# Each token's gate halves as two accumulating products of 128 columns, evicted by a copy

## What is computed

```python
gate = jax.nn.softmax(top_s.astype(F32), axis=-1).astype(h.dtype)
...
act = jax.nn.gelu(jnp.einsum('tkd,td->tk', u[ix], hx), approximate=False) * gx
return jnp.einsum('tk,tkd->td', act, v[ix])
```

## Time and profile before

| | |
|---|---|
| median of 3 runs | 3873.95 us (3873.43 to 3877.39) |
| the profiled execution's own time | 3893.15 us |
| its span, first to last instruction | 3891.5 us |
| TensorE matmuls busy | 3833.1 us, 98% |
| TensorE weight loads busy | 3308.9 us, 85% |
| VectorE busy | 2804.0 us, 72% |
| ScalarE busy | 1878.9 us, 48% |
| GpSimd busy | 1667.1 us, 43% |
| the two gate stages | 729.2 to 1101.0 us and 2714.4 to 3097.1 us |

### The profile page before, as it was taken

One profiled execution on the slowest core, in us unless ns is written; L12 is line 12 of the kernel. 1 busy time (PEld: TensorE's weight loads), 2 busy tenths in 40 slices (PEclk: granted clock), 3 DMA queues, 4 the chain that ended last, 5 costly groups with the idle time before them and its releaser, 6 DMA issues.

```text
span 3891.5 us, 60334 instructions
## 1 busy us (share of the span) xinstructions
PE 3833.1 (98%) x18945; PEld 3308.9 (85%) x18945; DVE 2804.0 (72%) x5198; ACT 1878.9 (48%) x3594; POOL 1667.1 (43%) x1769
## 2 busy tenths in 40 slices
PE   9998999999999999999999999999999999999998
PEld 7665888888888999999788888888888888999997
DVE  4647799778742688887777774998777724778876
ACT  3747433577743333335555553333777733333334
POOL 0311335778720566651200001436877702556641
PEclk9999999999999999999999999999999999999999
DMA  9547466555556899994588873334555656999972
GB/s 275 170 150 191 163 208 202 196 197 187 192 211 203 295 359 362 356 352 145 173 237 236 241 211 114 106 122 154 204 187 191 223 198 215 344 339 360 363 279 92
DMA packets 547288, 875.95 MB, mean 225 GB/s; under 512 B 40593, under 2 KB 384785, under 8 KB 543281
## 3 DMA queue, kind: packets, MB, share of 16 engines
q1 hardware_dynamic: 458688, 605.81, 47.8%
q0 software_dynamic: 51568, 201.04, 14.0%
q10 hardware_dynamic: 36864, 67.13, 4.6%
HBM read 745.57 MB, written 262.21 MB: 259 GB/s over the span
## 4 chain that ended last, share of the span: by engine, by line
PE 86%; issue 5%; DVE 4%; ACT 3%; POOL 1%; another core or an unknown queue 0%; DMA 0%; ACTq 0%; DVEq 0%; SPq 0%; POOLq 0%
PE ps L191 77%; PE ps L1768 2%; ACT first_scaled L1787 1%; DVE own_sum L1636 1%; POOL w_lo L176 1%; PE ps L2332 1%; PE ps L2311 1%; ACT w_hi L163 1%; PE ps L1269 1%; PE ps L2082 1%; DVE w_lo L169 1%; PE ps L614 0%; PE ps L615 0%; PE ps L600 0%; DVE gate_group L1697 0%
## 5 line engine op out<-in xcount | busy, mean ns | idle before, releaser
L163 ACT ACTIVATE w_hi<-w_raw 128x1024 fp32r<-128x1024 f32 x692 | 732.3, 1059 | 1209.7 <-PE ps L191 891.8
L169 DVE TENSOR_TENSOR w_lo<-w_raw,w_hi 128x1024 fp32r<-128x1024 f32 x583 | 717.2, 1230 | 670.2 <-ACT w_hi L163 539.9
L191 PE MATMUL ps<-h_hi,w_hi 128*128 128x512 f32 (+1 forms) x3072 | 1155.9, 376 | 18.2 <-DVE w_lo L169 7.9
L191 PE MATMUL ps<-h_hi,w_lo 128*128 128x512 f32 (+1 forms) x3072 | 1143.3, 372 | 0.0
L191 PE MATMUL ps<-h_lo,w_hi 128*128 128x512 f32 (+1 forms) x3072 | 1142.0, 372 | 0.0
L191 PE MATMUL ps<-y_hi,w_hi 128*128 128x512 f32 (+1 forms) x2368 | 871.4, 368 | 8.2 <-DVE w_lo L169 6.4
L191 PE MATMUL ps<-y_hi,w_lo 128*128 128x512 f32 (+1 forms) x2368 | 867.9, 367 | 0.0
L191 PE MATMUL ps<-y_lo,w_hi 128*128 128x512 f32 (+1 forms) x2368 | 867.3, 366 | 0.0
L191 PEld LDWEIGHTS ps<-h_hi,w_hi 128*128 128x128 f32 x3072 | 577.9, 188 | 110.6 <-issue 13.2
L191 PEld LDWEIGHTS ps<-h_hi,w_lo 128*128 128x128 f32 x3072 | 577.7, 188 | 82.2
L191 PEld LDWEIGHTS ps<-h_lo,w_hi 128*128 128x128 f32 x3072 | 578.1, 188 | 78.5 <-issue 2.2
(11 more groups left out here) (376 smaller groups left out, 3555.4 us busy)
## 6 DMA issues: line engine op xcount, KB each, us to landing
value_rows<-in_v SPq DMA_DIRECT2D x256, 512.0 KB, 5.9
w_raw<-in_u SPq DMA_DIRECT2D x256, 512.0 KB
w_raw<-in_v SPq DMA_DIRECT2D x256, 512.0 KB
acts<-gelu ACTq DMA_DIRECT2D x256, 256.0 KB, 2.2
gates<-gate_group POOLq DMA_DIRECT2D x28, 2048.0 KB, 8.0
blocks<-acts SPq DMA_DIRECT2D x256, 192.0 KB
blocks<-gates SPq DMA_DIRECT2D x96, 512.0 KB
w_raw<-in_od_in SPq DMA_DIRECT2D x65, 512.0 KB
```

The lines of the kernel that those rows point to most:

```text
L163: self.nc.scalar.activation(self.wh[:, slot % SPL, :], self.raw[:, slot, :], ACT.Copy).then_inc(self.sig("w_hi_ready").sem, 1)
L169: self.nc.vector.tensor_tensor(self.wl[:, slot % SPL, :], self.raw[:, slot, :], self.wh[:, slot % SPL, :].bitcast(F32), ALU.subtract).then ...
L191: ins = self.nc.tensor.matmul(out, a[:, s, w], b[:, k, :], start=first and j == 0 and m == 0, stop=last and j == n - 1 and m == 2)
```

## The change

Each token's product of 256 columns becomes two products of 128 columns, one for each half, which accumulate in the same 128 columns of PSUM (`start` on the first, `stop` on the second). The second half of each token's place in PSUM stays unused. VectorE's eviction copies these 128 columns a token in place of adding 2 x 128. The semaphores, their counts and their order stay as they are.

```diff
@@ -1694,8 +1694,8 @@
             dve.wait_ge(gm.sem, g * TS + gm.base + R + 4 * q + 4)
             if at == 0:
                 dve.wait_ge(gd[half].sem, g * 32 + gd[half].base + 16 * (1 + part // 2))
-            v.tensor_reduce(gb[:, half, :, at:at + 4].rearrange("p a t -> p t a"),
-                            self.bank(q).rearrange("p t c a -> p t a c"), AX_X, ALU.add).then_inc(gc.sem, 1)
+            v.tensor_copy(gb[:, half, :, at:at + 4].rearrange("p a t -> p t a"),
+                          self.bank(q)[:, :, 0, :]).then_inc(gc.sem, 1)
 
@@ -1765,9 +1765,9 @@
                     pe.wait_ge(gc.sem, g * self.Q + gc.base + q + 1)
                     for r in range(4):
                         t = (4 * q + r) % R
-                        ins = p.nc.tensor.matmul(self.bank(q)[:, r, :, :].rearrange("p c a -> p (c a)"),
-                                                 self.o2[:, t, :], self.os[:, t, :, :].rearrange("p c a -> p (c a)"),
-                                                 start=True, stop=True)
+                        for c in range(2):
+                            ins = p.nc.tensor.matmul(self.bank(q)[:, r, 0, :], self.o2[:, t, :], self.os[:, t, c, :],
+                                                     start=c == 0, stop=c == 1)
                     ins.then_inc(gm.sem, 4)
```

## The result

The changed kernel takes **3947.55 us** (median of 4 runs, 3946.45 to 3950.55) against 3873.69 us before (4 runs). The ratio is 1.019, with a 95% interval of 1.0178 to 1.0202: 73.9 us slower, inside the forecast's range and its narrower one, and 5 us under the forecast of 3953. The profiled execution took 3947.13 us, its span 3945.5.

What follows compares the result with a forecast made beforehand. TensorE was taken to bound both gate stages, with 2.8 us idle; +80.6 us for the products less 2 us of waits made +79, so 3953 us against the 3873.95 median; range 3942 to 4128, its own narrower one 3943 to 3967.

Steps and rivals of the forecast that it cites:

- A: Gate products on TensorE: the weight load sets the narrow products' pitch, +69 to +93 us; chance 0.60.
- The load's pitch: Gate products on TensorE: 1,536 at 112 ns, 172.0 us, less 91.4 today, +80.6 us.
- The unit behind the burst: Next unit's wide products on TensorE, behind the longer burst: cost taken as already counted, no term of its own.
- The waits: TensorE's waits for the eviction in the gate stages: at most 2.8 us of idle time returns, 2 us taken off.
- Sum: Whole kernel: 80.6 - 2 = +79 us, forecast 3953 us against the median of 3873.95.
- VectorE: Gate evictions: a copy at 700 ns in place of 1,216, 99 us of VectorE time saved, all beside TensorE.
- The upper bound, 1,216: Gate eviction on VectorE: the copy's time bounded by 683 ns below and today's 1,216 ns above.
- B: Narrow gate products cost like plain float32 products, 224 ns each, +253 us or +237; chance 0.20.
- C: Second gate product finds its weights in place and pays no load, not slower, 3871 us; chance 0.07.
- D: Gate products' loads hide in part under the product before, pitch 86 ns, +41 us, 3915 us; chance 0.08.
- the 81 ns: Trainium skill's price per product for a stream of loads and products at N=128, an estimate of +33 us.
- E: As A, and TensorE's clock gives way; half the bursts at the lower level cost 86 us more, 4039; chance 0.05.

Runs made afterwards that it cites:

- e9: Changed kernel, but each gate product loads only 64 of the 128 stationary columns, same products and moving columns; ratio 1.0007 to the kernel before.
- e3: Changed kernel with only the first-half product of 128 columns for each token, second half left out; ratio 0.998 to the kernel before.
- e5: Kernel before with each token's product of 256 columns done twice into the same place; ratio 1.0228 to the kernel before.
- e6: Kernel before with four products of 64 columns for each token, side by side, added as before; ratio 1.0909 to the kernel before.
- e2: Kernel before with the eviction copying the first half in place of adding both halves; ratio 1.0002 to the kernel before.
- e1: Kernel before with two products of 128 columns for each token, side by side, VectorE still adding the halves; ratio 1.0193 to the kernel before.
- e7: Changed kernel, but the eviction writes its 512 values side by side; ratio 1.0186 to the kernel before.
- e8: e1 reordered to first halves of four tokens, then second halves, so no neighbours share weights; ratio 1.0188 to the kernel before.

## Why the prediction was right, and where its sum was off

Direction, cause and size held: the split pays a second full weight load per token on the engine that bounds. Load-bound (A) it is by e9, e3, e5 and e6 together: the average distance in a burst of 16 is 107 to 108 ns at 64 and at 128 columns with a full load, 119 at 256, and 60 at 128 columns with half a load. Step by step:

- **The load's pitch.** Taken 112 ns from plain float32 rows, and inside a burst it is 112. But the first product of a burst loads under a wide one, so the averages are 108.5, and 105 in a burst of eight. A pass has 13 units with eight tokens and 6 with four, so the six passes of both layers take 6 x (13 x 1.735 + 6 x 0.84) = 165.6 us in place of my 172.0. The term was too large by 6.
- **The unit behind the burst.** Not in my sum: it takes 5.52 in place of 5.48 us in 114 units, +4.6 us. This is the same load again, spared at the head of the burst and paid behind it, so the two errors nearly cancel, and counting 112 ns for every product came out almost right without my having seen either.
- **The waits.** I gave back 2 us, capped at the 2.8 us of idle time, and called them the eviction's. With the chain's own pieces (60 units of 5.48, the decode stage's last one, 45.7 us of gate products) a stage of before is 380.0 us, and it took 382.8: 2.8 us of waits a layer, 5.6 in all, twice the idle time of the earlier trace rows. So my cap of 2.8 us was no bound. The weight loads show more waiting than the matmul row; in the first stage before:

```profile
PEld ps L1768 <- DVE gate_group L1697: 2.3, 5, 0.6
PEld ps L191 <- DVE w_lo L169: 1.1, 2, 0.6
...
PE ps L1768 <- DVE gate_group L1697: 1.0, 3, 0.4
```

The columns are us, times and the longest. A third of the loads' waiting is not for the eviction but for `w_lo`, VectorE's share of the big product. After, the same sum gives 419.3 and the stage took 419.1, without any such wait: all of it is gone. And it is not the copy that removed it. e2 gives 1.1 us in the first stage and 1.0 in the second, and keeps the wait for line 169, while e1, with the old eviction, has the changed kernel's stages. The waits vanish since TensorE itself comes later. A slower bounding engine takes up the waits that it had.

- **Sum:** 165.6 - 91.4 + 4.6 - 5.6 = +73.2 us, where the two stages grew by 72.7.
- **VectorE.** This step failed: 1,119 ns and not 700, 192 x 0.097 = 19 us spared and not 99 (in the windows of the two stages VectorE's busy time fell by 21 us, where the prediction named some 100 as a sign). I argued that the old eviction's time was that of its reads, so that its stride cost nothing. The strided writes of 512 values take 1,119 ns by themselves, so taking reads away could spare no more than 97; how long the reads of 1,024 would take with writes side by side no run shows. The upper bound, 1,216, was the nearer row. The Trainium skill has it, in "SBUF — State Buffer", section "Door 1: The DMA port swizzle": accesses to SBUF that each cross into a new 16-byte line pay a penalty. Here every write did, and e7 agrees (1,120 against 680 ns). It cost nothing, as VectorE is covered.

Of the rivals, B (the price of plain float32, 224 ns) is refuted by every narrow run, C by e8, D by the pitch of 112, on average 108.5, in place of 86; the 81 ns that the prediction set beside D are not what this stream shows either. E was no fact of this change but of e6.

## What to carry to other kernels

Count a matmul by its weight load as well as by its columns: with 128 stationary columns of this type a product costs its load, 112 ns here, as long as its moving columns take less. On the line through 60 ns at 128 and 119 at 256 columns that is up to about 240 columns, an estimate. So splitting a product that just covers its load nearly doubles its price (119 to 217 ns), and merging two such halves that share their stationary operand gives the 98 ns back. Before sparing an engine, add up the bounding engine's pieces over the stage and compare with the stage's length; that difference, here 2.8 us of 383, is all that sparing another engine can give. And when the reads of an instruction are halved, ask what its writes take.

## What was not expected of the hardware

A narrow product costs about the same beside wide ones (125 ns) as in a burst (112): it is through in 60, and the product behind it pays the rest. Runs of 32 products of 64 columns, 3.6 us and more, brought the granted clock to 0.50 at many of them and made the next 24 wide products slower by a quarter (7.04 against 5.55 us), while bursts of 16 products of 128 columns, 1.74 us, left it at 1.00. A copy of 512 values from PSUM with writes 128 bytes apart takes 1,119 ns, side by side 680.
